# Sample attention of a hybrid decoder step: an output chunk ahead of the scores, weight parts ahead of softmax, idle products in the waits

## What is computed

```python
def dilated_sample(q, k_all, v_all, rel_bias, window, dil, wbuf):
    ...
    s = jnp.einsum('bthd,btmhd->bhtm', q, kg) * ATTN_SCALE + bias[:, None, :]
    p, lse = masked_softmax_stats(s, valid[None, None])
    o = jnp.einsum('bhtm,btmhd->bthd', p, vg)
    return o, jnp.transpose(lse, (0, 2, 1))

def merge_out(oa, ob, r, a_out_g, gla_out_g, w_out, dtype):
    ...
    oa = rmsnorm(oa, a_out_g).reshape(B, T, MIX_A)
    ob = rmsnorm(ob, gla_out_g).reshape(B, T, MIX_B) * jax.nn.silu(r.astype(jnp.float32))
    return jnp.concatenate([oa, ob], axis=-1).astype(dtype) @ w_out
```

## Time and profile before

| | us |
|---|---|
| median of 3 runs | 1544.39 |
| lowest and highest run | 1542.82, 1545.78 |
| profiled execution: span, and its own time | 1544.0, the same 1544.0 |
| TensorE busy with matmuls | 1514.8 (98%) |
| VectorE busy | 875.7 (57%) |
| ScalarE busy | 633.9 (41%) |
| GpSimd busy | 52.4 (3%) |
| bytes moved by DMA | 370.98 MB, mean 240 GB/s |

### The profile page before, as it was taken

The page is one execution under the profiler, slowest core; times in us unless marked ns, Lnnn a source line. Parts: engine busy times, 40 slices in busy tenths (PEclk is TensorE's granted clock), DMA queues, the critical chain, the costliest instruction groups (busy, mean ns, idle before and its releaser), DMA issues.

```text
span 1544.0 us, 27862 instructions
## 1 busy us (share of the span) xinstructions
PE 1514.8 (98%) x11762; PEld 1372.8 (89%) x11762; DVE 875.7 (57%) x1509; ACT 633.9 (41%) x873; POOL 52.4 (3%) x89
## 2 busy tenths in 40 slices
PE   8999999999999889999999999999999999999999
PEld 4877888888888557768899999999999999999999
DVE  3655676666667435557454555555554565656574
ACT  3433444434445215235333333334333445545453
POOL 2000000001111000000000000000000000000000
PEclk8999999999999999999999999999999999999999
DMA  9998777777777997997644444454545444454541
GB/s 354 400 355 346 307 257 257 257 259 267 255 288 270 413 414 309 422 363 292 251 164 164 164 164 169 159 184 147 188 146 182 163 172 178 166 181 172 178 176 53
DMA packets 62283, 370.98 MB, mean 240 GB/s; under 512 B 7431, under 2 KB 7913, under 8 KB 27081
## 3 DMA queue, kind: packets, MB, share of 16 engines
q1 hardware_dynamic: 56096, 351.08, 60.6%
q0 software_dynamic: 5904, 17.93, 3.4%
q10 hardware_dynamic: 162, 0.22, 0.0%
HBM read 359.32 MB, written 9.88 MB: 239 GB/s over the span
## 4 chain that ended last, share of the span: by engine, by line
PE 89%; DMA 5%; DVE 3%; SPq 2%; ACT 1%; issue 1%; POOL 0%; ACTq 0%; DVEq 0%
PE ps L989 26%; PE ps L990 25%; PE ps L991 25%; PE ps L941 4%; PE ps L934 1%; SPq L710 1%; DMA ring<-in_w_ada_early 1%; DMA ring<-in_w_out 1%; DMA ring<-in_cache_k_win 1%; DMA proj<-in_tables 1%; ACT whi L1501 1%; DVE wlo L2028 1%; PE ps L1321 1%; DMA ring<-in_w_ada 1%; PE ps L1290 1%
## 5 line engine op out<-in xcount | busy, mean ns | idle before, releaser
L989 PE MATMUL ps<-hhi,whi 128*128 128x288 f32 x3136 | 934.0, 298 | 3.1 <-DVE wlo L1871 1.6
L990 PE MATMUL ps<-hlo,whi 128*128 128x288 f32 x3136 | 922.6, 294 | 0.0
L991 PE MATMUL ps<-hhi,wlo 128*128 128x288 f32 x3136 | 922.5, 294 | 0.0
L989 PEld LDWEIGHTS ps<-hhi,whi 128*128 128x128 f32 x3136 | 589.0, 188 | 38.8 <-issue 29.9
L990 PEld LDWEIGHTS ps<-hlo,whi 128*128 128x128 f32 x3136 | 589.2, 188 | 0.7
L991 PEld LDWEIGHTS ps<-hhi,wlo 128*128 128x128 f32 x3136 | 588.9, 188 | 0.0
L1492 ACT ACTIVATE whi<-ring 128x1024 fp32r<-128x1024 f32 x178 | 185.7, 1060 | 200.7 <-PE ps L991 200.7
L1864 DVE TENSOR_TENSOR wlo<-ring,whi 128x1024 fp32r<-128x1024 f32 x178 | 212.0, 1221 | 78.8 <-ACT whi L1492 78.4
L2028 DVE TENSOR_TENSOR wlo<-ring,whi 128x1024 fp32r<-128x1024 f32 x96 | 117.0, 1223 | 79.6 <-ACT whi L1501 79.5
L1501 ACT ACTIVATE whi<-ring 128x1024 fp32r<-128x1024 f32 x96 | 100.8, 1053 | 130.1 <-PE ps L991 114.2
L2545 DVE TENSOR_TENSOR wlo<-ring,whi 128x1024 fp32r<-128x1024 f32 (+1 forms) x94 | 105.7, 1132 | 56.2 <-ACT whi L1805 56.2
(11 more groups left out here) (298 smaller groups left out, 905.4 us busy)
## 6 DMA issues: line engine op xcount, KB each, us to landing
ring<-in_w_up SPq DMA_DIRECT2D x88, 1024.0 KB, 4.8
ring<-in_w_down SPq DMA_DIRECT2D x32, 1408.0 KB, 6.1
ring<-in_w_ada SPq DMA_DIRECT2D x42, 1024.0 KB, 6.8
ring<-in_w_in SPq DMA_DIRECT2D x28, 1024.0 KB, 6.5
ring<-in_w_ada_early SPq DMA_DIRECT2D x22, 1024.0 KB, 7.5
proj<-in_w_ada SPq DMA_DIRECT2D x22, 1024.0 KB, 11.0
ring<-in_w_in_early SPq DMA_DIRECT2D x20, 1024.0 KB, 9.3
ring<-in_w_out SPq DMA_DIRECT2D x16, 1024.0 KB, 13.2
```

Source lines behind the costliest of these rows:

```text
L989: mm(out, w_hi, x_hi, start=start, stop=False)
L990: mm(out, w_hi, x_lo, start=False, stop=False)
L991: return mm(out, w_lo, x_hi, start=False, stop=stop)
```

## The change

Six edits, all in the four groups of sample attention:

1. TensorE: `out_product(3g)` of groups 1 to 3 runs ahead of the group's scores instead of behind them.
2. TensorE: idle products. One in each group ahead of `probabilities`, behind a new wait until VectorE has taken the output rows of the group before; one behind each of the seven score units 0 to 6 of group 3; two ahead of each of the tiles 3 and 4 of the values of group 2. That is 15.
3. ScalarE: `out_hi(3g+2)` ahead of the exponential instead of behind it.
4. ScalarE: the copy of the output rows ahead of `out_hi(3g+4)` instead of behind it.
5. VectorE: `out_lo(3g+2)` directly behind the maximum, ahead of the scaling (and of the next queries).
6. SyncE: the load of slab 2 (chunks 4 and 5) two cache units earlier.

```diff
@@ SyncE
             out_half(1)
-            cache_loads(9, 32)
+            cache_loads(9, 30)
             out_half(2)
+            cache_loads(30, 32)
             out_half(3)
@@ TensorE, values(g)
                 for t in range(KT):
+                    if g == 2 and t >= 3:
+                        idle_products(4, 2)
                     for b in range(2):
                         pe.wait_ge(*unit_landed(value_place(g, t, b)))
@@ TensorE, the groups
             for g in range(NB // 2):
+                if g:
+                    out_product(3 * g)
                 scores(g, 8)
                 scores(g, 9)
                 new_scores(g)
@@
                     scores(g, n)
-                if g:
-                    out_product(3 * g)
+                    if g == 3 and n < 7:
+                        idle_products(7 if n >= 4 else 6, 1)
                 out_product(3 * g + 1)
+                pe.wait_ge(*SU.upto("out", g - 1))
+                idle_products(6, 1)
                 probabilities(g)
@@ ScalarE
             for g in range(NB // 2):
+                out_hi(3 * g + 2)
                 softmax(g)
-                out_hi(3 * g + 2)
                 probabilities(g)
                 out_hi(3 * g + 3)
+                output(g)
                 out_hi(3 * g + 4)
-                output(g)
@@ VectorE
                 maxima(g)
+                out_lo(3 * g + 2)
                 norm_scores(g)
                 if g < NB // 2 - 1:
                     queries(g + 1)
                 if g == 3:
                     out_tiles(4)
-                out_lo(3 * g + 2)
```

## The result

The changed kernel takes 1548.13 us, median of 16 runs (1545.37 to 1549.95), against 1544.07 of the kernel before in the same session (16 runs, 1542.52 to 1545.78): ratio 1.0027, interval 1.0021 to 1.0034. It is 4.1 us **slower**, by more than the 0.2% that I could have called a change. I had forecast 1543.7 with 5% for slower, and the result lies above the range.

The account below looks back on a forecast made before the run. DMA transfers were taken to bound the groups, with group 3's last values landing near 591.28 and only 0.96 us of slack. 1544.0 - 0.7 = 1543.3 profiled, with 0.4 to the median 1543.7 us; range 1540.5 to 1546.0.

Parts of the forecast that it names:

- Waits removed: Groups 0 to 2: waits of 5.1 us (group 1) and 1.1 us (group 0) go; TensorE newly waits 4 us in group 2.
- this costs nothing at the end: Group 2, TensorE's 4 us wait for the scaling: no cost, since the values cannot end before their last unit lands.
- Chunk 3g ahead of the scores: Group 3: scores still end at 577.0, values start at 584.9 instead of 588.70, then TensorE waits for cached values until 591.4.
- Idle products at nothing: Groups: the 15 idle products lie where TensorE waits anyway; 0.3 to 0.5 us each if uncovered, taken as 0 in all.
- The rows nearest to their places are waits: Reason for taking the 15 idle products at 0, out of between 0 and 7 us for all.
- the gain of 0.7: End of group 3: chunk 12 begins at 593.4 instead of 594.12, 0.7 us sooner.
- Everything behind moves with it.: Behind the groups: all work after chunk 12 shifts by the same 0.7 us, giving 1543.3 for a profiled execution.
- The starting point: Whole kernel: 1544.0 taken as the profiled execution before, with 0.4 us between it and the median of the runs.
- TensorE is the bound after all: Rival, group 3: last values are there when TensorE comes, so it keeps 3.8 us: 1540.6; chance 12%.
- The clock falls in the last values: Rival, group 3: thin waits drop the clock to 1.2 GHz, chunk 12 pays 1.4 us: 1545.1; chance 12%.
- The queue runs dry at slab 8: Rival, behind the groups: slab 8's load waits for chunk 13's lower part, up to 5.1 us late: 1548.8; chance 3%.
- The chances: Whole kernel: forecast 68%; faster by more than 3.1 us 0.17, slower by more 0.05, within 0.78.

Follow-up runs that it names:

- 40 short: Changed kernel with its 15 idle products replaced by 40 short ones (32 columns), 25 of them added in group 3's scores: 1546.63 us, ratio 1.0018 to the kernel before.
- none and slabs first: Changed kernel without any idle product and with the first two w_ada slabs issued ahead of output slab 10: 1544.53 us, ratio 1.0002 to the kernel before.
- none: Changed kernel without any idle product, all moves of the order kept: 1545.51 us, ratio 1.0009 to the kernel before.

## Why the prediction was wrong, step by step

- *Waits removed.* Right: the 5.1 us of group 1 and the 1.1 us of group 0 are gone, and group 2 waits 3.5 us for the scaling (I said 4). None of it reached the end. But "this costs nothing at the end" left out the clock behind that wait: the values of group 2 began 1.3 us later than before, and with them went the cover of the four idle products there.
- *Chunk 3g ahead of the scores.* Right for the order alone: 593.22 for chunk 12 (said 593.4), two new waits, last values at 591.23 (said 591.3). But the gain can't be told from the spread between executions: kernels with the order of before began chunk 12 anywhere from 593.24 to 594.12.
- *Idle products at nothing.* **Wrong twice.** "The rows nearest to their places are waits" held for the order before. Chunk 9 ahead of the scores lets the keys pile up, so my own step took away the cover of the next: seven products of 0.6 us, twice the 0.3 that I had as the lower bound and above the 0.5 of the upper one, put the scores' end at 581.03 where I had 577.0. The seven alone did not do it: chunk 9 had begun 1.4 us late, since the four in group 2 had lost their wait too. These are 4.0 us on TensorE. By my steps it had 3.1 us to spare there (values from 584.9 and 5.4 us for them and the new rows, 590.3, against 593.4 by the landing); the other 0.9 ate the gain of 0.7.
- *"Everything behind moves with it."* **The step that failed.** It made no price for the number of instructions. 60 instructions more moved a 16 KB packet into the first w_ada slab, where one of its 16 shares came 1.6 us late and the wait grew by 1.9 us, and with the wait came the clock, 2.3 us: 4.2 us on a path where I had zero. The stretch of 607 to 616 that I read the earlier trace rows has a DMA share of 0.31, and I stopped there; from 616 to 624 it is back at 0.96, and the waits for w_ada, 1.8 us in the kernel before, stood in the list of waits of which I quoted only four.
- *The starting point.* The 0.4 us added to the profiled execution set a span beside a time (see above). It did no harm: the forecast is the old median less 0.7 either way.
- *The rivals.* "TensorE is the bound after all": in the changed kernel it had no slack in group 3, but only since the idle products filled it, and the time of 1540.6 never came. "The clock falls in the last values": absent in the changed kernel, seen in three of the five traces with such waits. Its price of 1.4 us was met where the clock fell behind the new rows (40 short: chunk 12 1.5 us longer). Where it fell at the last values it was more, since these and the new rows are slow too (1.94 and 1.93 for 1.06 each): from the last values to the end of chunk 12 it is 8.4 us with none and slabs first (591.88 to 600.25) and 5.3 with none (591.23 to 596.49), 3.1 us. The Trainium skill (TensorE: Matmul & The Clock Gate, HAM oscillation) describes a kernel whose bursts of matmuls, about 2 us each, were shorter than the DMA waits between them, and each burst began at the low clock. Its waits were 3 to 5 us; here waits of 1.2 to 1.4 us between bursts of 1.06 us were enough, but not in every trace. "The queue runs dry at slab 8": not seen, no wait for it, and the one for a lower part behind chunk 13 is 0.50 us (0.49 before).
- *The chances.* 0.05 for slower rested on one named mechanism; a kernel with 1.8 us of waits at a full queue just behind the changed stretch deserved more.

What stays open: the packet takes one DMA engine for about 1 us, and the share was late by 1.6; no run tells where the other 0.6 comes from. The packet was never moved without changing the number of instructions. That it carries TensorE's instructions follows from its coming at the same number of them in all 13 kernels, and from its label; no view names the engine it serves. And no run shows what decides whether the clock falls behind a wait of 1.4 or 1.8 us: the code up to the last values is the same in the two kernels without idle products, and it held in one trace and fell in the other.

## What to carry to other kernels

In this kernel added instructions were not free of charge even inside a wait: they moved the fetch of later instructions, which held up one share of a slab of data. So look at every place behind the edit where an engine waits for a slab by less than a microsecond or two, and give that slab room first; here the place of two loads in the plan gave more than the whole change. And when a step fills idle time, take the cover of the following steps from the timeline with that step in it, not from the one before.

## What was not expected of the hardware

The instruction packet: 16 KB each, one for every 252 matmuls and weight loads of TensorE on average, and 0.95 to 1.3 us long in the place that counts here. In the nine kernels with the slabs in their old place, the first wait was 1.89 to 2.25 us in the three where it came between 620 and 624 us, and 0.37 to 0.56 us in the six where it came before 616 or after 628. In the three, the last of the slab's 16 shares landed 1.5 to 1.6 us behind the 15th; in the six, at most 0.12. And 25 additional products made a kernel faster by 2.9, 4.1 and 3.4 us in three pairs, and by 0.8 in the fourth, where they stood on TensorE's path (by the ratios, but for the 4.1, whose two kernels ran side by side).
